# More products of constants on TensorE ahead of norms, head norms, the first input product and in two routing heads

## The reference, cut to what matters

```
def rmsnorm(x, g):
    y = xf * lax.rsqrt(jnp.mean(xf * xf, axis=-1, keepdims=True) + EPS)
    return (y * g).astype(x.dtype)

def hgrn2_readout(o, g, norm_g):                     # and the same form in gla_heads: the head norms
    return rmsnorm(o, norm_g).reshape(b, n, HG_VAL) * jax.nn.silu(g)

def moe(h, router_w, router_b, w_gate, w_up, w_down): # twice: 512 tokens, then 256
    scores = jax.nn.sigmoid(t @ router_w)             # 16 experts in 4 groups
    ...                                               # best group, the two best experts in it, their weights
    y = (jax.nn.silu(t @ wg) * (t @ wu)) @ wd         # summed over experts with those weights

def even_mixer(hc, hl, w_in, ...):                    # the first input product is hl @ w_in, hc @ w_in
    pl = hl @ w_in
```

## Time and profile before

| | us |
|---|---|
| three runs, median (lowest to highest) | 2987.56 (2985.0 to 2988.52) |
| the profiled execution's own time | 2985.41 |
| its span, first to last instruction | 2983.3 |
| TensorE busy with products | 2710.9 (91%), 14667 rows |
| VectorE / ScalarE / GpSimd busy | 1758.4 / 1318.6 / 254.0 |
| mean granted TensorE clock | 0.955 |

### The profile page before, as it was taken

The page is one execution under the profiler, slowest core; times in us unless marked ns, Lnnn a source line. Parts: engine busy times, 40 slices in busy tenths (PEclk is TensorE's granted clock), DMA queues, the critical chain, the costliest instruction groups (busy, mean ns, idle before and its releaser), DMA issues. The chain is left out here.

```text
span 2983.3 us, 38461 instructions
## 1 busy us (share of the span) xinstructions
PE 2710.9 (91%) x14667; PEld 2106.2 (71%) x14667; DVE 1758.4 (59%) x2733; ACT 1318.6 (44%) x2065; POOL 254.0 (9%) x234
## 2 busy tenths in 40 slices
PE   6999888969999979998799988999899899888998
PEld 4666566857888857888643337878678788877786
DVE  3799878448999966455510006546555545557554
ACT  3323264337888854342210005435454444446443
POOL 1000036001111010024000000002100000110000
PEclk8999989989999989999899999999999999989999
DMA  6556500229997132330579985543145454420542
GB/s 274 213 211 218 205 1 1 91 106 350 414 414 284 53 141 71 113 114 1 191 295 410 412 325 182 179 140 135 57 162 203 149 190 171 159 102 12 193 178 78
DMA packets 94501, 536.90 MB, mean 180 GB/s; under 512 B 10864, under 2 KB 12272, under 8 KB 70640
## 3 DMA queue, kind: packets, MB, share of 16 engines
q1 hardware_dynamic: 87408, 509.45, 45.7%
q0 software_dynamic: 6768, 24.64, 2.3%
q10 hardware_dynamic: 144, 0.35, 0.0%
HBM read 599.94 MB, written 22.54 MB: 209 GB/s over the span
## 5 line engine op out<-in xcount | busy, mean ns | idle before, releaser
L1274 PE MATMUL ps<-w_hi,x_hi 128*128 128x512 f32 x1136 | 451.2, 397 | 7.5 <-DVE x_lo L2984 3.9
L1276 PE MATMUL ps<-w_hi,x_lo 128*128 128x512 f32 x1136 | 444.7, 391 | 0.0
L1275 PE MATMUL ps<-w_lo,x_hi 128*128 128x512 f32 x1136 | 444.1, 391 | 0.0
L1274 PEld LDWEIGHTS ps<-w_hi,x_hi 128*128 128x128 f32 x1136 | 214.8, 189 | 51.6 <-DVE w_lo L2966 4.5
L1276 PEld LDWEIGHTS ps<-w_hi,x_lo 128*128 128x128 f32 x1136 | 214.4, 189 | 46.1
L1275 PEld LDWEIGHTS ps<-w_lo,x_hi 128*128 128x128 f32 x1136 | 214.9, 189 | 42.9
L1274 PE MATMUL ps<-w_hi,hidden_hi 128*128 128x512 f32 x536 | 210.8, 393 | 7.8 <-DVE hidden_lo L2971 6.0
L1274 PE MATMUL ps<-x_hi,w_hi 128*128 128x512 f32 (+1 forms) x512 | 202.1, 395 | 9.8 <-DVE w_lo L847 9.0
L1276 PE MATMUL ps<-w_hi,hidden_lo 128*128 128x512 f32 x536 | 209.1, 390 | 0.0
L1275 PE MATMUL ps<-w_lo,hidden_hi 128*128 128x512 f32 x536 | 208.8, 389 | 0.0
L1275 PE MATMUL ps<-x_lo,w_hi 128*128 128x512 f32 (+1 forms) x512 | 195.4, 382 | 0.0
(11 more groups left out here) (718 smaller groups left out, 5888.2 us busy)
## 6 DMA issues: line engine op xcount, KB each, us to landing
weights_A<-in_moe_gate SPq DMA_DIRECT2D x132, 512.0 KB
weights_B<-in_moe_up SPq DMA_DIRECT2D x132, 512.0 KB
weights_A<-in_ffn_gu SPq DMA_DIRECT2D x24, 2048.0 KB, 8.1
weights_B<-in_ffn_gu SPq DMA_DIRECT2D x20, 2048.0 KB, 8.1
weights_C<-in_moe_down SPq DMA_DIRECT2D x66, 512.0 KB
weights_D<-in_moe_down SPq DMA_DIRECT2D x66, 512.0 KB
weights_C<-in_ffn_down SPq DMA_DIRECT2D x24, 1024.0 KB, 7.1
second_weights<-in_moe_gate SPq DMA_DIRECT2D x44, 512.0 KB
```

Source lines behind the costliest of these rows:

```text
L1274: nc.tensor.matmul(out, w_hi, x_hi, start=first, stop=False)
L1275: nc.tensor.matmul(out, w_hi, x_lo, start=False, stop=False)
L1276: return nc.tensor.matmul(out, w_lo, x_hi, start=False, stop=last)
```

## The change

Five kinds of places get further products of constants: 2 at the start of each `rms_norm`, 5 at the start of each `head_norm_gate`, 8 at the start of `even_in`'s stage, and in both routing heads 14 at the start, 8 ahead of the wait for `mask_done`, 30 ahead of the wait for `rows_made`. That is 8 + 10 + 8 + 104 = 130 products. In the heads one wait is new: before the 8, TensorE waits until ScalarE has copied all turned rows out of PSUM (`h_copied`), since these products write bank 0, which held some of them. Nothing else is changed.

```
@@ rms_norm
                 def _(pe):
+                    self.stay_awake(3, 2)
                     for k in range(chunks):
@@ even_in
+                    self.stay_awake(0, 8)
                     for p in range(NPIECE):
@@ experts, and the same in expert_pairs
                 def _(pe):
+                    self.stay_awake(0, 14)
                     pe.wait_ge(s["w_in"], 48)
...
                     for t in range(1, nt):
                         turn_rows(t)
+                    pe.wait_ge(s["h_copied"], 2 * nt)
+                    self.stay_awake(0, 8)
                     pe.wait_ge(s["mask_done"], 1)
...
                     last.then_inc(s["counted"], 1)
+                    self.stay_awake(0, 30)
                     pe.wait_ge(s["rows_made"], 1)
@@ head_norm_gate
                 def _(pe):
+                    self.stay_awake(6, 5)
                     for j in range(pairs):
```

## The result

The changed kernel took 2996.25 us in the median of 19 runs (2990.79 to 3000.59), the kernel before 2988.18 in the median of 19. The ratio is 1.0022, 95% interval [1.0015, 1.0029]: slower by 0.2%. The forecast was 2983.5 with a range of 2976 to 2990; it was wrong in sign. The profiled execution of after took 2997.50 us (span 2995.4), that of before 2985.41 (span 2983.3). They differ by 12.1 us, because that execution of before lay 3.2 us under its kernel's mean and that of after 2.3 above, so a difference between these two profiles overstates the change.

The account below looks back on a forecast made before the run. TensorE was taken as busy 91% of the span, so only short half-clock stretches could gain. The terms 0 - 1.5 - 1.5 - 2 + 1 = -4.0 us, set against the median 2987.56, gave 2983.5 us, range 2976 to 2990.

Parts of the forecast that it names:

- Input product: At the first input product, 8 products delay the first piece but the clock recovers sooner: 0, bounds -1 to +1.7 us.
- Norms: At the four norms, 2 products each make one slow norm in four fast: -1.5 us, bounds -5 to +1.
- Head norms: At the two head norms, faster sums against late blocks of 5: -1.5 us for both, best -5.0, worst +2.6.
- the saving of 3.3 and 1.7 us on the sums: In the two head norms, two-column sums at full clock take 0.116 us a row instead of 0.218.
- First head: In the first routing head, faster logits, counts and token sums bring the gather sooner: -2 us, bounds -4.5 to +2.5.
- second +1: In the second routing head, gather unmoved, turn and loop start at half clock: +1 us, bounds -0.5 to +3.
- `who_done` comes about 2.4 us earlier: In the first routing head, the token numbers are ready about 2.4 us sooner, and the gather with them.
- Nothing moves that landing: In the second routing head, the copy of `h` lands unchanged behind 12 weight pieces, so the gather still starts at 1494.24.
- The average over executions: Over the whole kernel, clock edges fall elsewhere each execution: averaged -4 us, against about -5.5 by the profiled edges alone.
- The signs that I had set: Wrong if the second head's gather moves, a 30 ends later than `rows_made`, or counts still take 4 us or more.
- The rival of -11.5 us: The clock holds at every place: norms -3.5, head norms -4, first head -4, second 0; 2977, chance 0.25.
- late blocks: Blocks begun at half clock outlast the events they wait beside, decided at the 30s: +9 us, 2996, chance 0.08.

Follow-up runs that it names:

- short_two_rows_first: Kernel before with 4 products at the input product, 2 at each head norm and the copies of `h` ahead of the last four weight pieces: 0.9997, -0.9 us.
- The parts alone: Kernel before with one part added each: norms -0.4, input product +2.2, head norms +3.0, heads' 14s +2.7, 30s +1.5, 8s -1.7 us.

## Why the prediction was wrong, point by point

- **Input product, forecast 0, bound +1.7: +2.2 ± 0.8.** The block's length (3.75 us) and the late start (1.6) were as worked out. The gain set against them ("the clock starts to recover 1.8 us sooner") was real too, and put low: at the 30th product 0.3 us of the delay were left on average. The step that failed is that the term ends there. The clock fell again 17 to 20 us behind the opening, as it had in before, and then stayed low for 10.2 to 13.7 us in the six profiles with the 8 products, 6.8 to 10.2 in the fourteen others. That is most of the 1.9 us of the table. Why it stays low for longer there is open.
- **Norms, forecast -1.5: -0.4 ± 0.7.** Giving "one norm in four" the full 1.74 us was too much: the slow one went from 5.30 to 4.76 us (4.78 where the norms were alone), a third of the 1.74 us.
- **Head norms, forecast -1.5: +3.0 ± 0.8.** I had both ends in hand, -5.0 and +2.6, and took a value near the middle of them. The step that failed is the saving of 3.3 and 1.7 us on the sums, priced at 0.116 us a row. The narrow sums stayed at half clock (0.213) with five products ahead of them, in both places and in every kernel that had them. The delay was larger than put, 1.6 us and not 1.3: the first sum stood 2.28 us behind ScalarE's first square (1415.13 - 1412.85) where it had stood 0.68 behind it, and in the second head norm likewise. A part came back in the products behind the sums, so that the next stage opened 0.7 and 1.3 us later on average. The rest of the 3.0 isn't located.
- **First head, forecast -2, second +1: together +4.7 ± 0.9.** Right: logits, token sums, the counts under 4 us, the 30 late by up to 2 us if the clock falls under the counts, the turn. "`who_done` comes about 2.4 us earlier" fails against the one profile of before (31.00 and 30.88 us from opening to gather) but holds in size over all profiles, where the gather is 2.1 us sooner. The loop behind it gives back 1.1 and not 0.4, so the first head stands at -1.0. The size is off, and not the sign.
- **Second head's gather: right in what releases it, wrong in "Nothing moves that landing".** It is still released by the copy of `h`, with `who_done` 3.3 us earlier for nothing and turn and loop at 0.50. But the gather came 1.3 us later behind the opening, and 1.6 later over the profiles. The turn lost 0.9 as priced, and the first nine rows of the loop 0.1, since they had been at half clock before too. The forecast of +1 has become +2.7 in the profiles. What the heads lost beyond that isn't located.
- **Not in the sum at all:** the fourth norm's own closing block, 3 us late in after. I priced the blocks that are added, and not the old ones behind them, whose cover rests on the clock at which they run. Why the clock falls there just in the kernels with all 26 products outside the heads isn't settled.
- **The average over executions.** The Trainium skill ("TensorE: Matmul & The Clock Gate", section "What's actually happening") has the activity check run on its own beat. From it I took that the edges fall anywhere, and averaged. At the input product the profiles bear that out: the clock rose 4.9 to 6.9 us behind the opening in the eleven that have no block there. Elsewhere they show few outcomes: from the second norm to the first head 16.6 us in most kernels and 17.5 in two; in the first head with the same code 30.9 us to the gather, or 33.2 to 33.8. There an average should be one over the outcomes that occur, and one profile gives only one of them. What draws one or the other is open.
- **The signs that I had set.** Two came: the second head's gather moved, and a 30 ended later than `rows_made`, in the first head by 1.8 us and in the second by 0.5. The third, counts of 4 us or more, did not (3.77).
- **Slips of the working.** The clock came back 3.9 us behind the start of the 14 products (665.6), and not 4 to 6; the 9.5 us worked out from it for the block of 30 were near the 9.64 measured. The rival of -11.5 us gives 2976, and not 2977.

The parts alone add to -0.4 + 2.2 + 3.0 + 2.7 + 1.5 - 1.7 = +7.3, against +6.6 measured; by their errors (about 1 each, so 2 to 3 in all) that agrees, though short_two_rows_first shows that such sums can be off by more.

Of the rivals "late blocks" gave the right time (2996, chance 0.08), in part by luck: the input product and the head norms measured a little over the upper bounds that it took for them, the one for a reason that it hadn't named, and its deciding place, the 30s, was not where the time went.

## What to carry to other kernels

Size a block of filler for the clock at which it starts, not for full clock: where TensorE had just stood idle here, 8 products of constants took 3.75 us and not 1.9, and half of the block or less costs nothing where the whole one costs 2 to 3 us. Don't stop at the block's own event: at the input product the delay was made up within 30 products, and the time went in a fall of the clock some 14 us behind the block. Read several profiles before you explain 2 us: the first head alone differed by 3 us between kernels in which its code is the same. Price what stands behind it too, the older fillers first, and look for what the gain waits on: here a copy behind twelve pieces of weights on a DMA queue. Four pieces moved behind it were worth about 3 us, while 104 products beside it lost 4.7.

## What the runs showed that I had not expected

- Under the two-column sums the clock did not come back: 32 rows at 0.213 us each, 6.8 us with TensorE busy without a break, at half clock to the end in all 20 profiles. Under the 128-column products of the first head's 30 in after it did, 5.7 us behind their start (651.5 to 657.2).
- The clock fell under the 16-column counts of after too, at 650.3, though 8 full products at full clock stood right ahead of them; in before there were none.
- The clock also fell under the 32-column rows of `w_dt` in the input product's stage, with TensorE busy without a break, in all 20 profiles.
- The copy of `h` was issued 8.2 us behind the second head's opening in after and 9.7 in before, with the same queue and bytes, and yet the gather that it releases came 26.3 and 25.1 us behind it. An earlier issue behind the same twelve pieces brought nothing. Why it landed even a little later isn't settled.
